# Hybrid decoder layer on one core: in the attention loop, the transposes of a slot are issued ahead of the value products of the slot before it

## The reference, cut to what matters

```
# cmp: compressed keys (at most 63)
p_cmp = masked_softmax(qc @ k_cmp.T - slope * dist, dist >= 0);  o_cmp = p_cmp @ v_cmp
imp = p_cmp @ ov                    # importance of each block of 64 keys
idx = top_k(score(imp), 8)          # which blocks the selected branch sees
# selected: keys of the chosen blocks, up to the query itself
p = masked_softmax(qc @ ks.T - slope * dist, dist >= 0);         o_slc = p @ vs
# window: the last 256 keys
p = masked_softmax(qc @ kw.T - slope * dist, window);            o_win = p @ vw
o = g0 * o_cmp + g1 * o_slc + g2 * o_win
```

## Time and profile before

| what | value |
|---|---|
| median of 2 runs | 1152.39 us (1150.3 to 1154.48) |
| profiled execution | 1149.09 us, of which its span is 1147.3 us |
| attention in the span | from about 304 to 652 us |
| TensorE busy | 1094.6 us, 95% of the span |
| VectorE busy | 654.4 us, 57% |
| ScalarE busy | 321.7 us, 28% |
| granted TensorE clock, mean | 0.983 of full speed |

### The profile page before, as it was taken

One profiled execution on the slowest core, in us unless ns is written; L12 is line 12 of the kernel. 1 busy time (PEld: TensorE's weight loads), 2 busy tenths in 40 slices (PEclk: granted clock), 3 DMA queues, 4 the chain that ended last, 5 costly groups with the idle time before them and its releaser, 6 DMA issues.

```text
span 1147.3 us, 14732 instructions
## 1 busy us (share of the span) xinstructions
PE 1094.6 (95%) x4873; PEld 663.4 (58%) x4874; DVE 654.4 (57%) x1479; ACT 321.7 (28%) x798; POOL 157.4 (14%) x193
## 2 busy tenths in 40 slices
PE   6999999999999999999999899999957999999995
PEld 3544574445566878888777787555533444444442
DVE  3321224433354666775565299445379788887983
ACT  3311121211233554555444555323210000000000
POOL 0020211300000030000000030000003233333332
PEclk9999999999999999999999899999978999999998
DMA  6310041102000100000000230522417888899332
GB/s 241 114 42 0 1 108 57 37 14 77 1 3 2 55 25 4 2 3 4 1 1 1 103 118 15 193 101 110 166 73 264 299 302 290 317 380 345 125 101 84
DMA packets 74176, 119.77 MB, mean 104 GB/s; under 512 B 14368, under 2 KB 53376, under 8 KB 74120
## 3 DMA queue, kind: packets, MB, share of 16 engines
q1 hardware_dynamic: 63032, 88.08, 22.7%
q0 software_dynamic: 11088, 30.95, 7.7%
HBM read 105.90 MB, written 21.50 MB: 111 GB/s over the span
## 4 chain that ended last, share of the span: by engine, by line
PE 65%; DVE 6%; issue 1%; ACT 0%; POOL 0%; DVEq 0%; POOLq 0%; ACTq 0%
PE ps L1745 14%; PE ps L1115 10%; PE ps L2005 10%; PE ps L1084 9%; PE ps L1755 8%; PE ps L1099 5%; PE ps L1130 3%; PE ps L1070 1%; PE ps L2025 1%; PE ps L1089 1%; PE ps L2015 1%; DVE big_u L1533 1%; DVE big_w L1577 1%; PE ps L1417 1%; DVE big_u L1529 1%
## 5 line engine op out<-in xcount | busy, mean ns | idle before, releaser
L1577 DVE STREAM_TRANSPOSE big_w<-big_w 32x256 f32<-32x256 f32 x400 | 174.3, 436 | 30.3 <-DMA big_w<-hn_dram,misc 23.8
L1745 PE MATMUL ps<-ring_gate_up,big_w 128*128 (+1 forms) x400 | 181.3, 597 | 2.5 <-DVE big_w L1577 2.5
L511 PE MATMUL ps<-big_w,big_u 128*128 128x512 f32 (+1 forms) x448 | 173.8, 542 | 0.0
L1238 DVE TENSOR_REDUCE big_w<-ps 128x2 f32<-128x768 f32 (+15 forms) x96 | 78.2, 815 | 107.6 <-PE ps L1089 88.2
L511 PEld LDWEIGHTS ps<-big_w,big_u 128*128 128x128 f32 x448 | 83.7, 191 | 75.5 <-issue 69.4
L1745 PEld LDWEIGHTS ps<-ring_gate_up,big_w 128*128 128x128 f32 x400 | 74.6, 192 | 87.7 <-issue 87.7
L1187 ACT ACTIVATE big_u<-ps 128x512 f32<-128x512 f32 (+7 forms) x160 | 75.6, 514 | 176.4 <-PE ps L1099 176.4
L1084 PE MATMUL ps<-ring_down,misc 97*128 97x512 f32 (+3 forms) x320 | 119.1, 481 | 2.0 <-ACT ring_gate_up L1197 2.0
L1115 PEld LDWEIGHTS ps<-ring_down,big_u 128*128 128x128 f32 x912 | 109.1, 192 | 15.5 <-issue 12.3
L2005 PE MATMUL ps<-big_w,big_u 128*128 128x512 f32 x256 | 114.7, 595 | 0.9 <-ACT big_u L2148 0.9
L1115 PE MATMUL ps<-ring_down,big_u 128*128 128x65 f32 x912 | 114.3, 274 | 0.9 <-ACT big_u L1187 0.9
(11 more groups left out here) (348 smaller groups left out, 1281.9 us busy)
## 6 DMA issues: line engine op xcount, KB each, us to landing
ring_gate_up<-in_w_gate SPq DMA_DIRECT2D x16, 1024.0 KB, 9.9
ring_gate_up<-in_w_up SPq DMA_DIRECT2D x16, 1024.0 KB, 12.7
ring_down<-in_w_down SPq DMA_DIRECT2D x16, 1024.0 KB, 15.3
misc<-in_x SPq DMA_DIRECT2D x16, 512.0 KB, 3.4
big_w<-in_w_in SPq DMA_DIRECT2D x6, 1024.0 KB, 7.8
big_w<-in_w_out SPq DMA_DIRECT2D x8, 512.0 KB, 5.0
hn_dram<-big_u SPq DMA_DIRECT2D x8, 512.0 KB, 2.6
out<-ring_gate_up SPq DMA_DIRECT2D x8, 512.0 KB, 3.7
```

The costliest lines, as they stand in the source:

```text
L511: last = nc.tensor.matmul(ps[:, b, 0:width], uT[:, k, c * P:(c + 1) * P], wbuf[:, n % 2, k, 0:width], start=(k == 0), stop=(k == KD - 1))
L1238: ins = nc.vector.tensor_reduce(neg[:, br, h0:h0 + len(heads)], src, AX.X, ALU.max, negate=True)
L1577: last = nc.vector.transpose(dst[j * 32:(j + 1) * 32, :, i * 32:(i + 1) * 32], src[i * 32:(i + 1) * 32, :, j * 32:(j + 1) * 32])
L1745: last = nc.tensor.matmul(ps[:, 2 + b, :], xT[:, b, k, :], ring_gu[:, bass.ds(at + k * 2 * D_EXP, BANK)], start=(k == 0), stop=(k == KD - 1))
```

## The change

The call of `transposes(j - 1)` moves ahead of `values(j - 2)`. Nothing else is changed: the same instructions with the same waits are issued on every engine; only TensorE's order differs. The pieces of the z product stay where they were: the second half of a step's pieces now comes behind the transposes and the value products.

```
@@ -1137,6 +1137,8 @@
                 scores(j)
             if j in piece_at:
                 z_pieces(piece_at[j][0], piece_at[j][1])
+            if 1 <= j <= J:
+                transposes(j - 1)
             if j == J + 1:
 
                 pe.wait_ge(o_read, len(groups) - 1)
@@ -1145,8 +1147,6 @@
                 values(j - 2)
             if j in piece_at:
                 z_pieces(piece_at[j][1], piece_at[j][2])
-            if 1 <= j <= J:
-                transposes(j - 1)
             if j in sel_at:
                 selection(sel_at[j])
```

## The result

The changed kernel took 1174.12 us (two runs, 1173.22 and 1175.03) against 1152.39 before. The ratio is 1.0178, 95% interval [1.0112, 1.0245]. A second series of the same kernel on another occasion gave 1173.17 us against 1151.12, ratio 1.016 [1.0091, 1.0229]. (The times given are medians. The ratios and their intervals are estimated from all runs of both kernels, and the quotient of the two medians can differ from them by 0.3%: here it is 1.019.) The change is slower by 1.6 to 1.8%, within the 2% that I forecast as likeliest, at the upper part of the range; the predicted 1166 was 8 us too low. The profiled execution took 1173.22 us, its span 1171.5, 24.2 more than before.

What follows compares the result with a forecast made beforehand. TensorE, busy 95%, was taken as the bound. Stalls of 13.8 us in late and 3.2 in earlier units, less 1.7 won, gave +15.3 us: 1164.4 or 1167.7, stated as 1166, range 1151 to 1179.

Steps and rivals of the forecast that it cites:

- The bound and the cover: Attention: TensorE, busy 95%, has few gaps to win back; moved transposes lose one set of values, 1.1 to 1.8 us cover.
- The chain through ScalarE: Every attention step: copy and exponentials move forward with the transposes, so the loop stays as long; cost 0.
- The rival in which every step waits: ScalarE's exponentials start no earlier, 0.28 us wait per ordinary slot: 1181 or 1185 us; chance 0.10.
- First stall: Six units: first window slot's last two transposes wait for the bank until VectorE writes the selection's rows; about 1.15 us each.
- Second stall: Late units: first selected slot's transposes wait for its late maximum and exponentials; 1.0, 1.2, 1.25 us for seven, six, five blocks.
- Earlier units: Three units ahead of the late ones stall through VectorE's list, 3.2 us in sum; other early units 0.
- 1.05: Stall in us in an earlier unit where VectorE has three small state-space steps behind a reading; slots 19 to 28.
- 1.35: Stall in us at the first selected slot of the unit in front of the first choice; slots 38 to 43.
- The 0.85: Stall in us in another earlier unit with VectorE's three small state-space steps behind a reading; slots 28 to 38.
- What is won: TensorE gaps filled: 0.7 us at the z pieces' end, 0.4 at a selection, 0.6 in the second last step; 1.7 total.
- The clock: TensorE's granted clock stays at 1.00, as stalls of at most 1.4 us are shorter than a harmless 2.01 us gap.
- the third rival: Each of some twelve stalls brings half clock for 4 us, 24 us lost in all: 1190 us; chance 0.03.

Runs made afterwards that it cites:

- both_new: Changed kernel with late units' queries moved to the third selected slot's step and GpSimd's weight scaling delayed behind the last selection: 1152.11 us, ratio 1.0006.
- s1_back: Changed kernel with the old order restored in one step per unit, the transposes of the first selected slot: 1170.31 us, ratio 1.0151.
- three_places: Kernel before with the new order only in the z-piece steps, the last selection's step and the last step with transposes: 1153.73 us, ratio 1.0006.
- ends_only: Kernel before with the new order only in the z-piece steps and all steps from the last CMP slot on: 1149.68 us, ratio 0.9963.
- w1_back: Changed kernel with the old order restored in one step per unit, the transposes of the first window slot: 1165.09 us, ratio 1.0107.
- rows_first: Changed kernel with VectorE writing the selection's rows ahead of half the queries instead of behind them: 1165.34 us, ratio 1.0108.
- queries_moved_new: Changed kernel with VectorE's query transposes for units 10 to 15 moved from two window steps to the third selected slot's step: 1159.92 us, ratio 1.006.
- pool_late_new: Changed kernel with GpSimd's scaling of the output weights waiting for the last selection's rows: 1168.34 us, ratio 1.0129.
- change_again: Changed kernel run once more with no edit, against the kernel before: 1173.17 us, ratio 1.016.

## Why the prediction was right or wrong

**The bound and the cover: right.** TensorE had nothing to win but a few gaps, and one set of values of cover was too much to give up.

**The chain through ScalarE, cost 0: right for the whole change.** both_new shows it: every step in the new order, 1.0006. The rival in which every step waits fell with it. Where the orders meet it is not always right. After a switch from old to new, only one set of scores stands between two sets of transposes, and the stall shrinks as that set gets longer: in s1_back 0.35, 0.25 and 0.14 us with five, six and seven key blocks, and none with eight, at the last selection in three_places. The last step, with no scores at all, had the 1.80. ends_only's switch, at the short CMP slot of unit 15, cost nothing.

**First stall: right.** 1.15 us in six places forecast, 1.00 to 1.01 in six places measured, ended by line 1299.

**Second stall: right in mechanism, mixed in size.** Forecast 1.0 to 1.25 in each late unit; 1.04, 1.04, 0.86 and 0.67 in four of them. In the two units in which the clock fell (behind the gaps that end at 547.9 and 574.4) there was none: TensorE came later by itself. Its slower matmuls took the place of the wait. So two short falls cost less than their length says: those units lost 2.9 and 2.8, the others 2.1 to 2.6. s1_back, which has no stall at S1 that could give way, bears this out: its three late units with a fall lost 3.2 to 3.3 us, two without one 1.6, so there a fall of 3.4 us cost half its length. Per unit 2.3 us were forecast and 2.5 measured.

**Earlier units: the sum right by accident, one size wrong.** 3.2 us were forecast and 3.7 measured, the clock left out. 1.05 was 0.9 and 1.35 was 0.7. The 0.85 was a gap of 2.16, some 2.0 of time, because I read VectorE's small steps from the old trace at 0.20 to 0.22 us each; beside GpSimd's scaling they took up to 1.09. The trace of before had the warning, a step of 0.69 instead of 0.43 in the same stretch, but I didn't look at GpSimd.

**What is won: too low.** 1.7 forecast, 2.3 measured (1.0 + 0.5 + 0.8).

**The clock: this step failed.** I wrote that a gap of 2.01 us behind 0.6 of transposes had done no harm, that mine were shorter, and gave the fall 0.03. The sum has nothing for the clock. The sign that I had named for the third rival, a granted clock below 1.00 between 370 and 640 us, came; its size, twelve falls and 24 us, did not. The long fall behind 2.16 us took about 8.4 us: 10.5 lost in slots 28 to 38, less the 2.0 that w1_back lost there with a gap of 1.99 and no fall. That is about the whole error of 8 us; the other misses nearly cancel, so that the measured time still came out inside the stated range. One case in which the clock held was no bound. With gaps of nearly the same length in the same place it fell in four profiles (at 2.16, 2.07, 2.14 and 2.16) and held in one (1.99). In two of the four (rows_first and queries_moved_new) it fell inside the gap, 1.3 and 1.1 us after the gap's start, so the length of the gap alone does not decide it.

The short falls tell more of what makes it fall. In the four profiles that have the bank's gap of 1.0 us (the change twice, s1_back and pool_late_new, six such gaps each, 24 in all) a fall began 1.4 to 2.6 us behind it 11 times. Behind the gaps at S1, as long but with 128-row values of 1.4 us and more after the transposes, it never did. (Twice one of 6.8 us began at the gap of 0.78 near 379, ahead of W2's transposes in the short slots.) The bank's gap lies inside transposes and has the CMP values behind it, with at most 63 rows; the gaps at S1 have scores ahead of them and transposes only behind. The Trainium skill (TensorE: Matmul & The Clock Gate, Part 4) says that transposes don't count as TensorE activity in the way matmuls do. By that rule this stretch (0.60 us of transposes, a gap of 1.0, 0.37 of transposes) is one idle stretch, and the runs agree in so far as w1_back and rows_first, without that gap, had no fall in a late unit. The other 13 of the 24 had no fall, and no run here shows why. That the thin CMP values take part is only argued; no run here changed them alone.

## What to carry to other kernels

Before an instruction is moved ahead on the busiest engine, list what its inputs pass through on the other engines, with their whole lists of work in order, and compare the end with the new place; an engine that is half idle on average can be the one that is late in a few steps. Where two orders meet, work that covered a latency is missing, so look at each switch: here the wait behind it was from nothing (ends_only, the one version that won) to 1.8 us. And price a stall with the clock behind it, above all one that lies among transposes; here 13 us of gaps became 22 us of time, 8.4 of them by one clock fall.

## What was not expected of the hardware

GpSimd working on 128x1024 float32 in SBUF (2.8 us a piece) stretched some small VectorE steps beside it from 0.16 to 0.22 us up to 0.55 to 1.09, and left others as they were (line 1324 took 0.23 between them). The Trainium skill (GPSIMD Engine Reference, 1. Specifications) names contention for the SBUF interfaces that GpSimd shares with VectorE, for VectorE instructions with two SBUF inputs or in a two-port mode; lines 1260 and 1328 have two inputs, and so has 1324, which was spared; line 1326, which was hit, has one. And the granted clock is not a function of the gaps alone: the same kernel's two profiles have nearly the same gaps and falls in different places, and three profiles (change_again, pool_late_new and ends_only) have a fall of 3.4 us that begins between 306 and 316 us, in the z pieces. The only gap ahead of it in attention is the one of 0.86 at attention's start, which every profile has, and in two of the three that had ended 10 us before.
